# Two-layer SSM, attention and mixture-of-experts trunk: the overflow test goes ahead of the last unit, the expert scratch moves out of the ring and 1.5 MB more of weights take its place, the last piece is cut into column halves, and the unit matrix is loaded first

## The reference

```python
h2 = rms_norm(x, norm2_g[l])
glog = xt @ w_group + b_group                       # 4 groups; the best one
elog = (xt @ w_expert + b_expert)[best group]       # 8 experts of it; the best two
y[token] += weight * ((silu(gate) * up) @ w_down[e])      # gate, up = split(xb @ w_gate_up[e], 2)
x = x + y
```

## Time and profile before

| | us |
|---|---|
| median of 3 runs (lowest, highest) | 1356.83 (1356.13, 1358.35) |
| the profiled execution, its own time | 1356.94 |
| its span, first to last instruction | 1355.1 |

### The profile page before, as it was taken

One profiled execution on the slowest core, in us unless ns is written; L12 is line 12 of the kernel. 1 busy time (PEld: TensorE's weight loads), 2 busy tenths in 40 slices (PEclk: granted clock), 3 DMA queues, 4 the chain that ended last, 5 costly groups with the idle time before them and its releaser, 6 DMA issues.

```text
span 1355.1 us, 18227 instructions
## 1 busy us (share of the span) xinstructions
PE 1165.5 (86%) x7390; PEld 522.2 (39%) x7391; DVE 418.4 (31%) x840; ACT 181.1 (13%) x373; POOL 171.1 (13%) x186
## 2 busy tenths in 40 slices
PE   7999999988977877686799999999798767787687
PEld 5455555424322332232264555554243212332232
DVE  5799532311101110011087894332021001100011
ACT  1422412100000000000015124130000000000000
POOL 1756400000000000000035672000000000000000
PEclk9999999998988888899899999999999888887988
DMA  8433657799999999999963326759999999999997
GB/s 279 166 125 125 249 240 298 317 428 388 429 428 428 429 428 429 428 428 427 414 222 146 115 113 249 328 230 384 426 398 427 428 430 426 429 429 427 430 423 304
DMA packets 64935, 462.31 MB, mean 341 GB/s; under 512 B 20616, under 2 KB 20720, under 8 KB 38512
## 3 DMA queue, kind: packets, MB, share of 16 engines
q1 hardware_dynamic: 64096, 461.44, 82.3%
q10 hardware_dynamic: 784, 0.09, 0.0%
HBM read 460.47 MB, written 1.05 MB: 341 GB/s over the span
## 4 chain that ended last, share of the span: by engine, by line
PE 53%; DMA 33%; DVE 6%; SPq 4%; issue 2%; ACT 1%; DVEq 0%; ACTq 0%
DMA pool_all<-in_w_gate_up_dram 30%; PE ps L1045 16%; PE ps L814 8%; PE ps L1059 5%; PE ps L848 4%; PE ps L873 4%; DMA pool_all<-in_w_down_dram 3%; SPq L517 3%; PE ps L987 3%; PE ps L1010 2%; PE ps L693 2%; PE ps L829 2%; PE ps L712 1%; PE ps L727 1%; PE ps L784 1%
## 5 line engine op out<-in xcount | busy, mean ns | idle before, releaser
L1045 PE MATMUL ps<-pool_all 128*32 128x512 f32 (+1 forms) x2816 | 360.3, 671 | 126.4 <-DMA pool_all<-in_w_gate_up_dram 126.4
L1045 PEld LDWEIGHTS ps<-pool_all 128*32 128x32 f32 x2816 | 95.7, 122 | 383.8 <-issue 383.3
L1059 PE MATMUL ps<-pool_all 128*32 128x512 f32 (+1 forms) x1408 | 164.6, 621 | 24.8 <-DMA pool_all<-in_w_down_dram 18.7
L1803 DVE SCALAR_TENSOR_TENSOR pool_all<-pool_all,ps 128x512 f32<-128x512 f32 x22 | 15.1, 687 | 500.3 <-ACT pool_all L1365 500.3
L814 PE MATMUL ps<-pool_all,hT 128*128 128x512 f32 x256 | 114.3, 598 | 0.0
L1365 ACT ACTIVATE pool_all<-ps 128x512 f32<-128x512 f32 x22 | 13.1, 597 | 644.3 <-PE ps L1045 644.3
L987 PE MATMUL ps<-pool_all,hT 128*128 128x128 f32 x704 | 89.0, 287 | 10.7 <-issue 10.5
L987 PEld LDWEIGHTS ps<-pool_all,hT 128*128 128x128 f32 x704 | 84.5, 200 | 30.7 <-issue 30.7
L1059 PEld LDWEIGHTS ps<-pool_all 128*32 128x32 f32 x1408 | 45.9, 114 | 129.0 <-issue 127.6
L2059 POOL TENSOR_TENSOR pool_all<-pool_all 128x512 f32<-128x512 f32 x64 | 80.0, 1286 | 25.1 <-DVE pool_all L1598 20.8
L1010 PE MATMUL ps<-pool_all 128*128 128x512 f32 x176 | 81.4, 605 | 0.0
(11 more groups left out here) (252 smaller groups left out, 988.2 us busy)
## 6 DMA issues: line engine op xcount, KB each, us to landing
pool_all<-in_w_gate_up_dram SPq DMA_DIRECT2D x110, 2048.0 KB, 28.8
pool_all<-in_w_down_dram SPq DMA_DIRECT2D x58, 2048.0 KB, 26.8
pool_all<-in_w_in_dram SPq DMA_DIRECT2D x14, 2048.0 KB, 13.0
pool_all<-in_w_gate_up_dram SPq DMA_DIRECT2D x24, 1024.0 KB, 15.5
pool_all<-in_w_gate_up_dram SPq DMA_DIRECT2D x24, 512.0 KB, 13.4
pool_all<-in_w_glu_dram SPq DMA_DIRECT2D x4, 2048.0 KB, 10.1
pool_all<-in_w_out_dram SPq DMA_DIRECT2D x4, 2048.0 KB, 11.9
pool_all<-in_w_down_dram SPq DMA_DIRECT2D x6, 1024.0 KB, 20.0
```

Of the source, the lines that this page charges most:

```text
L1045: mm = pe.matmul(ps[r, half], xT[:, k, r], lane_cols(n, TRIO * h, k % 4, half), start=(k == 0), stop=(k == KC - 1), skip_group_check=True)
L1059: mm = pe.matmul(ps[r, 2 + half], ffT[:, c, r], lane_cols(n, 2 * TRIO, c, half), start=(c == 0), stop=(c == 3), skip_group_check=True)
```

## The change

- **Scratch.** `xT` and the output buffer `ybuf` lie in the memory of x (`xs`), whose rows are already in PSUM and in `x_rows` when experts start. `back` shares memory with the routing masks, `act_buf` with the rope tables. What is left of the scratch takes the last quarter of slot 10.
- **Weights.** Three quarters of slot 10, 3072 columns or 1.57 MB, are loaded with the first k-rows of expert 31 right after slot 9. Slot 1 therefore takes rows of expert 4 (unit 2) while unit 0 still runs; only the last k-row of expert 31's first part goes to slot 1, and the last k-row of expert 4 waits for unit 1.
- **Test.** On all four engines the overflow test moves from behind unit 1 to ahead of unit 10. Unit 1 gathers for unit 2 like every other unit.
- **Last piece.** The fourth k-row of unit 10's w_down comes in two column halves, each with its own counter.
- **Start.** `ident` is loaded first, then x, then the two first loads of w_in, then the rest of the table.
- **GpSimd** in layer 1 waits until unit 10's activation is done before it writes the rope tables.

```diff
-    a_ = region(10 * SLOT)
-    xT = a_(1024).rearrange("p (k s) -> p k s", k=KC)
-    back = a_(256).rearrange("p (t s) -> p t s", t=NT)
+    a_ = region(10 * SLOT + 3 * D)
+    xT = xs.rearrange("p t (h c s) -> p t h c s", h=2, c=4)[:, :, 0]
+    ybuf = xs.rearrange("p t (h n) -> p t h n", h=2)[:, :, 1]
+    back = route_cols.rearrange("p (t s) -> p t s", t=NT)
+    act_buf = rope_cols
...
+        sp.dma_start(const("ident"), consts[:, 0:P]).then_inc(x_in, 16)
         sp.dma_start(xs, x.rearrange("o (t p) d -> p (o t) d", p=P)).then_inc(x_in, 16)
-        sp.dma_start(cst, consts).then_inc(const_in, 16)
...
+                sp.dma_start(cst[:, P:], consts[:, P:]).then_inc(const_in, 16)
...
             sp.dma_start(wide_slot(9), expert_part(l * EXPERTS + DUO, 0)).then_inc(landed[9], 16)
+            sp.dma_start(wide_slot(10)[:, 0:3], expert_part(l * EXPERTS + DUO + 1, 0)[:, 0:3]).then_inc(landed[10], 16)
...
-                for e, index in ((1, duo + 1), (0, duo if part else second), (2, second + 2)):
-                    load_piece(TRIO * part + e, index, a, b, landed[TRIO * part + e])
+                if n == 2:
+                    load_piece(1, duo + 1, 3, 4, landed[10])
+                for e, index in ((1, duo + 1 if part else second + 1), (0, duo if part else second), (2, second + 2)):
+                    load_piece(TRIO * part + e, index, a, 3 if n == 2 and e == 1 else b, landed[TRIO * part + e])
...
-            load_expert(1, second + 1)
+            load_piece(1, second + 1, 3, 4, landed[1])
...
                 for n, (a, b) in enumerate(((0, 2), (2, 3), (3, 4))):
+                    if part == 2 and n == 2:
+                        break
                     for e in range(TRIO):
                         load_piece(TRIO * part + e, last + e, a, b, tail_in[3 * part - 3 + n])
+            for half in range(2):
+                c = slice(512 * half, 512 * half + 512)
+                for e in range(TRIO):
+                    i = 2 * TRIO + e
+                    sp.dma_start(wide_slot(i)[:, 3:4, c], expert_part(last + e, i)[:, 3:4, c]).then_inc(tail_in[5 + half], 16)
...
-        pe.wait_ge(const_in, 16)
-        pe.wait_ge(x_in, 16)
+        pe.wait_ge(x_in, 32)
...
-            unit(1, 2, duo_lanes, alone=True, odd=True)
+            unit(1, 2, duo_lanes, odd=True)
+            pe.wait_ge(spared, at(spared, l, 2))
+            pe.sem_inc(settled, 1)
+            with pe.Fori(1, UNITS // 2) as j:
+                unit(j * 2, TRIO, trio_lanes(j * 2 - 1), turn=j)
+                unit(j * 2 + 1, TRIO, trio_lanes(j * 2, odd=True), turn=j, odd=True)
             pe.wait_ge(routed, at(routed, l, 1))
             pe.sem_inc(settled, 1)
             most = pe.value_load(ov_flag[0:1, 0:1], min_val=0, max_val=SEQ)
...
-            gather(main, 2)
-            pe.wait_ge(spared, at(spared, l, 2))
-            pe.sem_inc(settled, 1)
-            with pe.Fori(1, UNITS // 2) as j:
...
+            if l:
+                pool.wait_ge(main["h"], at(main["h"], l - 1, UNITS))
```

117 lines of the change are left out of this document (62 added, 55 removed).

## The result

The changed kernel takes 1349.39 us (median of 6 runs, 1347.06 to 1351.38) against 1356.70 (6 runs, 1356.12 to 1358.35) for the kernel before on the same chip: ratio 0.9944, 95% interval 0.9932 to 0.9956. It is faster by 7.3 us, not by 12.6, and 1.4 us above the range. The profiled execution took 1349.91 us, 7.03 less than that of before.

What follows compares the result with a forecast made beforehand. Two DMA-saturated stretches were taken to bound the kernel, so idle in the transfer queue before them counts. Layer 0 -3.7 -2.8 -0.2, layer 1 -3.7 -2.2 -0.2, start +0.2: -12.6 from 1356.9 gives 1344.3 us, range 1342.5 to 1346 (1342.3 to 1348.0 with rivals).

Steps and rivals of the forecast that it cites:

- The second hole: Queue running dry at 320 to 325 and 990 to 995 us; closing it was priced at 2.8 and 2.2 us.
- the first: Idle queue at 239 to 247 and 910 to 917 us; the early 1.57 MB there was worth 3.67 us per layer.
- the two terms: Per layer, 3.7 us for the early weights plus 2.8 (layer 0) or 2.2 us (layer 1) for the second hole.
- The tight issue: SP's issue of slots 6 and 7, expected within 0.3 us of 300.69 us, with 1 us of reserve.
- the two gains add, since they are different idle times of one queue: Weight queue: the early load's 3.67 us per layer and the second hole's 2.8 and 2.2 us were summed.
- the test ahead of unit 10 costs nothing: End of each layer: 5.28 us of PE idle, covered by 7.1 us of waiting; priced at nothing, range 0 to 2.
- The rule that the prediction set against the place: Before unit 10: a taken branch waits for its code by DMA, so the 5.28 us stall could differ there.
- each microsecond of idle removed moves the whole saturated stretch, and the layer's end with it: Second half of each layer: idle removed from the transfer queue ahead of the DMA-bound stretch counts in full.
- then ACT ends at about 15.0 and DVE goes on at 15.0: Start: the table lands at 14.7 us, so DVE's reciprocal comes at 15.0 instead of 14.8; +0.2 us.
- the upper bound that was kept for it: Start: +1.0 us, the upper bound on the start's term of +0.2 us; the lower was -1.1.
- the column halves: Unit 10's last w_down piece in two parts: 0.2 us per layer gained, bounds 0 and 1.
- the test is felt at the end: Rival, chance 0.13: the test before unit 10 outlasts its 7.1 us cover, 1 to 3 us per layer, 1346 to 1350.

Runs made afterwards that it cites:

- e1: The changed kernel with the rest of the constant table loaded right behind x, ahead of the first loads of w_in: 1348.05 us, ratio 0.9937.
- e2: The changed kernel with the last k-row of unit 10's w_down in whole pieces again, one counter: 1348.32 us, ratio 0.9937.
- e4: The changed kernel with the overflow test and its body taken out on PE, SP, ACT and DVE: 1348.66 us, ratio 0.9940.
- e7: The changed kernel with the old order of the start (x, the whole table, then w_in): 1348.00 us, ratio 0.9931.
- e9: The changed kernel with eps beside the unit matrix in the first load and the rest of the table behind all of w_in: 1345.17 us, ratio 0.9917.
- e5: The changed kernel with test, gather, start order and last piece undone; the scratch and the early 1.57 MB load stay: 1357.95 us, ratio 1.0004.
- e6: The changed kernel with early load, start order and last piece undone; the moved test and the scratch stay: 1354.38 us, ratio 0.9984.
- e8: The changed kernel with 1024 more idle wait instructions per layer on GpSimd, which ran ahead of the full queue: 1349.18 us, ratio 0.9944.
- e10: The kernel of e9 with the last k-row of unit 10's w_down in one piece again: 1346.47 us, ratio 0.9922.
- e13: The kernel of e9 with PE's loop over units 2 to 9 written as two loops: 1346.50 us, ratio 0.9916.
- e12: The kernel before with PE's loop over units 2 to 9 written as two loops: 1359.25 us, ratio 1.0014.
- e3: The changed kernel with the overflow test back behind unit 1, unit 2's gather still inside unit 1: 1350.97 us, ratio 0.9965.
- e11: The kernel before with ACT's unit loop cut behind unit 5 and 321 semaphore-counting instructions between the halves: 1356.88 us, ratio 1.0002.

## Why the prediction was half right

**Right: what bounds, and the bytes.** The second hole closed and the first was half filled, as described. Measured from unit 0, the transfers at 228 and 459 MB were 6.28 and 5.91 us ahead of before, against 6.5 and 5.9 forecast from the two terms (5.0 to 5.8 in layer 0 of e1, e2, e4, e7 and e9, whose unit 0 had no slow clock ahead of it). The tight issue came at 302.32 us, 1.6 us later than expected, and no hole opened at it.

**Right as a sum, wrong as it was said: "the two gains add, since they are different idle times of one queue".** They are not separate gains. e5 gives the first one alone: 0 instead of -7.4. e6 gives the second alone: -2.8 instead of -5.0. Bytes that are sent early are a gain only if no later wait has its own clock, and the second hole's end was set by PE. Only with the move is the load worth its bytes: 3.5 and 3.6 us per layer between e6 and the changed kernel.

**Right for this kernel, with little to spare: the test ahead of unit 10 costs nothing.** It was 6.13 us of idle in layer 0, not 5.28, and behind it the rows of gate and up waited for nothing; what covered it was the wait for w_down, 2.18 us. Without the test (e4) the lag was 0.11 and 0.17 us less. ACT's turn was ready 1.5 us ahead of the late landing, so of the 1.12 us of that landing only a part could have been had back with the test where it is: where the landing came earlier (e1, e8, e10, e13), the test's chain was the limit. The rule that the prediction set against the place, that the branch waits for its code, is seen in so far as a 16 KB transfer of PE's code lies in the idle time at both places (306.23 us before, 638.20 after); the idle time was 0.85 us longer at the new one.

**Wrong: "each microsecond of idle removed moves the whole saturated stretch, and the layer's end with it".** This step took the queue for one pipe. It is 16 engines, a load has landed when its last part has, and PE's code is fetched through the same engines. Shown: steps of 1.2 and 1.35 us at 16 KB transfers, which stay for up to 260 us (e12, e13), and the lag of w_down against the spread over 13 kernels. The last landing was spread over 3.64 and 3.61 us in place of 1.87 and 1.92, most of it from the fetches of the last 30 us, and gave back 1.12 and 1.02 us of the bytes' lead. It stays open why these fetches cost so much more than the one in the kernel before. The test's added ones are not needed for it (e4 has 637 and 659, 3.72 us of spread). That the holes had kept the engines level is not shown: the levelling of the second hole was undone by one fetch within 11 us.

**Wrong: "then ACT ends at about 15.0 and DVE goes on at 15.0".** The table was priced by bytes ahead of it, 14.7 us, and landed at 15.3; the larger part was missed altogether, since the 1.28 us load of ACT's function table was not in the list: before, it ran while DVE was busy, and the change put it behind the wait. +2.28 us on DVE, +1.03 at L638, the upper bound that was kept for it. Another 0.85 us of the +1.88 came from four matmuls (L923), told below. The two profiled executions overstate it: over six traces with the old start and five with the new one the start of unit 0 moved by 0.7 us, not 1.88 (e7).

**Mis-sized: the column halves.** L1072 took 10.04 and 9.87 us, not under 9.72 and 9.40, and from w_down's start to the last scatter 0.32 and 0.47 us were lost in place of 0.2 gained. The granted clock was 0.78 and 0.79 there, and 0.80 and 0.84 before; with the same halves e9 took 12.49 and 12.68 us at 0.88 and 0.84. So the clock may be the whole of it, but no run sets it apart.

Of the rivals, "the test is felt at the end" had the right size (1 to 3 us per layer) and place, and the wrong engine: not PE's cover, but the DMA engines.

## What to carry to other kernels

A hole in a full queue can be filled only up to the next wait whose end is set elsewhere: before pricing bytes sent early, follow the queue to the event that refills it, and price the edits one by one as well as together. Where PE waits for the last part of a load, look at the landings of all 16 parts, not only at the mean rate: a queue without pauses can keep a lag for hundreds of microseconds, and a fetch of code just ahead of the last landing may cost as much. Lay several executions side by side before a difference of a microsecond between two traces is put down to an edit. When a load moves behind others, list everything that stands behind its wait on the waiting engine, table loads too, and ask who needs only a few bytes of it: one column moved into the first load gave more (e9) than any order of the big ones that was tried (e1, e7), though the intervals of e9 and those two overlap.

## What the runs showed of the hardware that was not expected

- PE's instructions came as single transfers of 16 KB that held one DMA engine for mostly 1.0 to 1.1 us each, and for 0.9 to 1.9 us at the extremes (40 in the changed kernel); those of ACT and GpSimd as 8 KB in 0.31 us. The page of the changed kernel counts them:

```profile
q8 instruction: 40, 0.66, 0.2%
...
q14 instruction: 16, 0.13, 0.0%
```

  The Trainium skill (Runtime: NRT & Kernel Launch, Instruction fetch mechanics) says that a sequencer fetches the next 16 KiB block through a DMA queue of its own while it executes, and that this is mostly hidden. For PE the traces agree with the size; for ACT and GpSimd they show 8 KB, and the measurement decides. Hidden from PE is not free: what the transfers cost fell on the weights of the same DMA engine.
- With the queue full, the spread of 3.0 us at 1052 us was 3.05 us 180 us later (e12); a pause of a few microseconds brought it from 1.89 to 0.47 us, and one fetch back to 1.72 (the kernel before).
- PE's granted clock ahead of unit 0 was lower in three of the 15 profiled executions: 0.81 in the changed kernel, 0.71 in e3 and 0.67 in e11, a variant of the kernel before. Layer 0, 234 to 239 us, the changed kernel and then the kernel before:

```profile
234.00:239.00 5.00, 4.34 (x20) 2.73 (x20) 2.39 (x13) 3.80 (x6) 0.00 (x0) 0.81 0.96 367
```

```profile
234.00:239.00 5.00, 4.06 (x21) 2.76 (x22) 2.63 (x16) 4.68 (x6) 0.00 (x0) 1.00 0.87 367
```

  The mean of 0.81 lies between the two levels, 1.2 and 2.4 GHz. Since e11 has it too and e2 and e4 don't, it isn't the change's; why it falls in one execution and not in another, no run shows; four matmuls of L923 took 3.42 us there and 1.94 before. Unit 0 started at 244.4 us in e2 and e4, which have the same start, and at 245.53 here: 1 us of the profiled execution.
